# Expert routing made tile by tile, two routing tables, a gather issued one block earlier, and four edits in the first and the expert stage of a hybrid decoder layer

## The chip, the cores and the metric

One Trainium2 chip, one core of it. The metric is the device time of one execution in microseconds (us). TensorE is PE in the profile's rows, VectorE is DVE, ScalarE is ACT, GpSimd is POOL, and SyncE, which here only issues DMAs, is SP.

## What is computed

One decoder layer, 1024 tokens of width 1024, all float32. A recurrent branch and an attention branch share one input projection and one output projection; then each token goes to 4 of 32 experts.

```python
h = rmsnorm(x, ln1_w)
u, gate, q, k, v, f = split(h @ w_in)                      # 512, 512, 512, 512, 512, 8 columns
rec = rg_lru(conv4(u), ...) * gelu(gate)                   # a scan over the 1024 tokens
att = forgetting_attention(rmsnorm(q), rmsnorm(k), v, f)   # 8 heads of 64, causal
x = x + concat(rmsnorm(rec), rmsnorm(att)) @ w_out
h2 = rmsnorm(x, ln2_w)
top_vals, top_idx = top_k(h2 @ w_router + b_router, 4)     # of 32 experts
gates = softmax(top_vals)
for each expert e:                                         # over the tokens that chose it
    g = min(h2 @ w_gate_up[e][:, :1024] + b, 7)
    u = clip(h2 @ w_gate_up[e][:, 1024:] + b, -7, 7)
    x += gates * (((u + 1) * g * sigmoid(1.702 * g)) @ w_down[e] + b)
```

## The kernel before

The program is a row of blocks, one for each stage; a block ends when all its engines are done. Inside a block each engine has its own list of instructions, in the order in which the code is written, and they meet on semaphores (`wait_ge`, `then_inc`). `step(...)` issues an instruction and makes the same engine wait for its end.

**Stage A** (`stage_a`): the norm, the input projection in 20 chunks of 128 columns, and the recurrent branch. POOL issues 14 small DMAs for the parameters, then makes the identity and other constants (lines 188 to 215). PE waits for `consts` and all 14 DMAs before it transposes the parameters (line 543) and then the normed rows, 16 parts of 4 transposes, `turn(g)` (line 551), through two PSUM places. ACT takes each part as h_hi (line 267) and DVE as h_lo (line 411), and ACT's squares of the next row tiles stand between. Each product is three matmuls: hi with hi, hi with lo, lo with hi. From projection chunk 9 on `mean_squares` (line 579) sums the squares of a head pair, and behind chunks 10 to 13 `rec_squares` (line 586) adds up the squares of the four channel tiles of the recurrence with one float32 pair of matmuls each.

**Stage B** is the attention; the change does not touch it.

**Stage C** (`stage_c`): the output projection in 8 token tiles, the second norm and the router. PE: `project(t)`, `turn(t - 1)` (line 1121), `route(t - 2)` (line 1132), and at the end turn(7), route(6), route(7). DVE adds the residual (line 1076), scales to h2 (line 1081) and then adds the router's bias to the logits of tile t - 1 (line 1068), in one PSUM place.

**Stage D** (`stage_d`): the routing. DVE finds the best four experts of each tile (lines 1241 and 1242) and the choices as a 0/1 table (lines 1247 to 1250); PE counts them (lines 1331 to 1336). From the counts DVE works out how each expert's tokens are cut into work items of 256 down to 96 rows (classes of width), the experts' order (line 1277) and the list of items (line 1289), for which SP waits with the loads of the first expert's weights (six DMAs of 2 MB each). Then it finds the place of each token and builds, in 32 rounds, the two factors of a table (lines 1305 to 1308), whose products PE adds up (line 1342):

```python
            for q in range(TK):
                dve.tensor_scalar(one_lo[:, q, :], iota_lo[:], lo_f[:, q:q + 1], None, ALU.is_equal)
                dve.tensor_scalar(val_hi[:, q, 0, :], iota_hi[:], hi_f[:, q:q + 1], row_no[:, q:q + 1],
                                  ALU.is_equal, ALU.mult)
                dve.tensor_scalar(val_hi[:, q, 1, :], iota_hi[:], hi_f[:, q:q + 1], ex_q[:, q:q + 1],
                                  ALU.is_equal, ALU.mult).then_inc(lo_s, 1)
```

The sums are the token of each place (`rows_in`, line 1316) and its gate. Constants for all this come from POOL at the start of the block (line 1220).

**Stage E** (`stage_e`, once as E and once, only if numbers are out of range, as G): the experts. POOL clears `rows` (line 1547), copies two columns of `rows_in` (line 1522) and gathers 2 x 128 token rows by indirect DMA (line 1526). PE transposes them in four parts (line 1790), ACT and DVE split each part into x_hi and x_lo in float16 (lines 1594 and 1684), and weights are split alike, 256 columns at a time, into a ring of four (lines 1587 and 1664). Ahead of the loop ACT and DVE split four chunks of weights and then the four parts of the first rows. The loop has one body for each class of width, eight chunks of gate and up (lines 1823 to 1826) and four of down (line 1834) for each item; a weight slot is loaded again when its last use has gone.

## Time and profile before

| | us |
|---|---|
| median of 3 runs (lowest, highest) | 2110.95 (2109.69, 2113.56) |
| the profiled execution | 2106.65 |
| its span | 2104.9 |
| PE busy | 1938.3 |
| DVE busy | 1250.7 |
| ACT busy | 1049.5 |
| POOL busy | 400.0 |
| DMA | 501.73 MB, mean 238 GB/s |

An engine's busy time says how long it had an instruction in hand. Starts are given from the start of the span; a row of a timeline names in brackets how long its engine was idle before it, and what ended that. An idle engine costs something only where others wait for it.

### The profile page before, as it was taken

The numbers are of one execution on the slowest core, as the hardware profiler recorded it, in microseconds if no ns is written. First come the engines' busy times: TensorE is split into PE (matmuls) and PEld (weight loads), VectorE is DVE, ScalarE is ACT, GpSimd is POOL, SyncE is SP. The second block draws the span as 40 slices with busy tenths as digits, with TensorE's granted clock in tenths as the row PEclk, the third lists the DMA queues.
The fourth block names the chain that finished last, engine by engine and source line by source line (L and its number), as shares of the span: only waits on it lengthen the run. The fifth ranks groups of instructions, "written<-read, shape, count | busy, mean of one in ns | idle before, by whom it ended". The sixth has DMA issues, their size and how long they took to land.

```text
span 2104.9 us, 50349 instructions
## 1 busy us (share of the span) xinstructions
PE 1938.3 (92%) x20305; PEld 1790.2 (85%) x20305; DVE 1250.7 (59%) x2560; ACT 1049.5 (50%) x1444; POOL 400.0 (19%) x303
## 2 busy tenths in 40 slices
PE   6999998997964999999999999999999999998983
PEld 4777576786852999999999999999999999998982
DVE  4452345664247655555566667567868768677582
ACT  5464315552111444445555555556656566565561
POOL 4001000000002111111112211213324324233241
PEclk9999999998976999999999999999999999999996
DMA  4111102003429678888988899999999999999994
GB/s 136 41 40 40 31 2 80 1 1 133 151 78 327 201 268 279 276 277 290 306 300 271 287 300 337 336 337 299 354 372 359 367 370 355 370 363 361 370 352 119
DMA packets 251765, 501.73 MB, mean 238 GB/s; under 512 B 13024, under 2 KB 33808, under 8 KB 251584
## 3 DMA queue, kind: packets, MB, share of 16 engines
q1 hardware_dynamic: 231376, 446.73, 58.6%
q0 software_dynamic: 20256, 51.73, 11.3%
q10 hardware_dynamic: 48, 2.10, 0.3%
q8 instruction: 58, 0.95, 0.2%
q14 instruction: 27, 0.22, 0.0%
HBM read 471.16 MB, written 52.43 MB: 249 GB/s over the span
## 4 chain that ended last, share of the span: by engine, by line
PE 52%; DVE 4%; DMA 4%; issue 4%; SPq 2%; ACT 1%; POOL 0%; DVEq 0%; ACTq 0%; POOLq 0%
PE E_p_d L1834 22%; PE E_p_g L1823 5%; PE E_p_g L1826 5%; PE E_p_g L1825 5%; PE E_p_u L1826 4%; PE E_p_u L1823 4%; PE E_p_u L1825 4%; DMA E_w_st<-in_w_down 4%; DVE E_w_lo L1664 2%; PE E_p_t L1805 2%; PE E_p_t L1790 2%; SPq L1473 2%; ACT E_w_hi L1587 1%; DVE E_up L1724 0%; DVE E_gate L1712 0%
## 5 line engine op out<-in xcount | busy, mean ns | idle before, releaser
L1664 DVE SCALAR_TENSOR_TENSOR E_w_lo<-E_w_st,E_w_hi 128x2048 f16<-128x2048 f32 x260 | 594.6, 2287 | 61.8 <-ACT E_w_hi L1587 58.1
L1587 ACT ACTIVATE E_w_hi<-E_w_st 128x2048 f16<-128x2048 f32 x260 | 492.5, 1905 | 187.6 <-PE E_p_g L1826 98.6
L1834 PE MATMUL E_p_d<-E_a_f,E_w_st 128*128 128x160 f32 (+6 forms) x4096 | 537.0, 291 | 21.3 <-DMA E_w_st<-in_w_down 11.6
L1834 PEld LDWEIGHTS E_p_d<-E_a_f,E_w_st 128*128 128x128 f32 x4096 | 521.4, 193 | 29.3 <-DMA E_w_st<-in_w_down 12.6
L1823 PE MATMUL E_p_g<-E_x_hi,E_w_hi 128*128 128x160 f16 (+6 forms) x2048 | 373.1, 224 | 6.2 <-issue 6.2
L1823 PE MATMUL E_p_u<-E_x_hi,E_w_hi 128*128 128x160 f16 (+6 forms) x2048 | 371.7, 223 | 4.1 <-DVE E_w_lo L1664 4.1
L1825 PE MATMUL E_p_g<-E_x_lo,E_w_hi 128*128 128x160 f16 (+6 forms) x2048 | 373.1, 224 | 0.0
L1826 PE MATMUL E_p_g<-E_x_hi,E_w_lo 128*128 128x160 f16 (+6 forms) x2048 | 373.0, 224 | 0.0
L1826 PE MATMUL E_p_u<-E_x_hi,E_w_lo 128*128 128x160 f16 (+6 forms) x2048 | 371.7, 223 | 0.0
L1825 PE MATMUL E_p_u<-E_x_lo,E_w_hi 128*128 128x160 f16 (+6 forms) x2048 | 371.7, 223 | 0.0
L1536 POOL DMA_INDIRECT sum_rows<-E_y_rows,E_idx_out x66 | 169.1, 2562 | 598.7 <-ACT E_y_rows L1605 588.5
L1630 ACT ACTIVATE E_y_t<-E_p_d,E_bias 128x160 f32<-128x160 f32 (+6 forms) x256 | 81.7, 371 | 258.1 <-PE E_p_d L1834 258.1
L1823 PEld LDWEIGHTS E_p_g<-E_x_hi,E_w_hi 128*128 128x128 f16 x2048 | 201.0, 98 | 6.8 <-issue 6.7
L1823 PEld LDWEIGHTS E_p_u<-E_x_hi,E_w_hi 128*128 128x128 f16 x2048 | 200.4, 98 | 4.8 <-DVE E_w_lo L1664 4.8
L1825 PEld LDWEIGHTS E_p_g<-E_x_lo,E_w_hi 128*128 128x128 f16 x2048 | 201.0, 98 | 0.8
L1826 PEld LDWEIGHTS E_p_g<-E_x_hi,E_w_lo 128*128 128x128 f16 x2048 | 201.0, 98 | 0.1
L1825 PEld LDWEIGHTS E_p_u<-E_x_lo,E_w_hi 128*128 128x128 f16 x2048 | 200.4, 98 | 0.4
L1826 PEld LDWEIGHTS E_p_u<-E_x_hi,E_w_lo 128*128 128x128 f16 x2048 | 200.4, 98 | 0.0
L1703 DVE TENSOR_SCALAR E_bias<-bias 128x8 f32 x32 | 5.5, 172 | 285.6 <-ACT E_y_t L1630 283.4
L1526 POOL DMA_INDIRECT E_rows<-h_rows,E_idx_in x68 | 116.2, 1709 | 38.8 <-POOL E_idx_in L1522 28.5
L1712 DVE TENSOR_SCALAR E_gate<-E_p_g,E_bias 128x160 f32<-128x160 f32 (+6 forms) x256 | 79.5, 352 | 67.8 <-PE E_p_g L1826 67.8
L1622 ACT ACTIVATE E_sig<-E_gate 128x320 f32<-128x320 f32 (+6 forms) x128 | 54.8, 428 | 109.3 <-DVE E_gate L1712 108.1
(367 smaller groups left out, 2802.5 us busy)
## 6 DMA issues: line engine op xcount, KB each, us to landing
E_w_st<-in_w_gate_up SPq DMA_DIRECT2D x130, 2048.0 KB, 15.6
E_w_st<-in_w_down SPq DMA_DIRECT2D x64, 2048.0 KB
A_w_st<-in_w_in SPq DMA_DIRECT2D x20, 512.0 KB, 3.8
sum_rows<-C_x SPq DMA_DIRECT2D x10, 512.0 KB, 5.8
A_x_rows<-in_x SPq DMA_DIRECT2D x8, 512.0 KB, 8.6
B_wo_raw<-in_w_out SPq DMA_DIRECT2D x8, 512.0 KB, 3.2
C_x_res<-in_x SPq DMA_DIRECT2D x8, 512.0 KB, 4.2
x_rows<-C_x SPq DMA_DIRECT2D x8, 512.0 KB, 5.0
```

The lines of the kernel that those rows point to most:

```text
L1473: sp.dma_start(w_st[q][:], weights_of(a, e, q)).then_inc(w_in[q], 16)
L1526: pool.indirect_dma_start(rows[:, b, :], None, m.h2_d, bass.IndirectOffsetOnAxis(ap=idx_in[:, b:b + 1], axis=0), bounds_check=token_max, o ...
L1536: pool.indirect_dma_start(m.sum_d, bass.IndirectOffsetOnAxis(ap=idx_out[:, b:b + 1], axis=0), y_rows[:, b, :], None, bounds_check=row_max, ...
L1587: act.activation(w_hi[c % RI][:], staged(c % NG), ACT.Copy, scale=SW).then_inc(hi_s, 1)
L1622: act.activation(sig[j % 2][:, :, 0:w], gate[j % 2][:, :, 0:w], ACT.Sigmoid, scale=ALPHA / S1).then_inc(sig_s, 1)
L1630: ins = act.activation(y_t[:, 2 * j + h, 0:w], p_d[j % 2][:, h, 0:w], ACT.Identity, bias=bias[:, 16 + 2 * j + h:17 + 2 * j + h], scale=1.0 ...
L1664: dve.scalar_tensor_tensor(out=w_lo[c % RI][:], in0=staged(c % NG), scalar=SW, in1=w_hi[c % RI][:], op0=ALU.mult, op1=ALU.subtract, accum_ ...
L1712: ins = dve.tensor_scalar(gate[j % 2][:, h, 0:w], p_g[j % 2][:, h, 0:w], bias[:, 2 * j + h:2 * j + h + 1], S1 * LIMIT, ALU.add, ALU.min)
L1823: pe.matmul(o_, wh, x_hi[:, k, 0:w], start=h == 0 and k == 0, stop=False, skip_group_check=True)
L1825: pe.matmul(o_, wh, x_lo[:, k, 0:w], start=False, stop=False, skip_group_check=True)
L1826: ins = pe.matmul(o_, wl, x_hi[:, k, 0:w], start=False, stop=k == KT - 1, skip_group_check=True)
L1834: ins = pe.matmul(banks[:, h, 0:w], staged(c)[:, k, h * P:(h + 1) * P], x[:, k, 0:w], start=h == 0 and k == 0, stop=k == KT - 1, skip_grou ...
```

## The change

In stage A: the identity is made first on POOL and has a semaphore of its own; the two DMAs for `b_forget` and the forget weights are no longer among those that the parameter transpose waits for; `turn(g)` uses four PSUM places; the squares of the recurrence are added on DVE and summed by one pair of matmuls behind chunk 13. In stage C: the choices are made tile by tile on DVE, two tiles behind; the router's PSUM place is doubled; route(6) stands ahead of turn(7); the routing constants are made on POOL here. In stage D: fewer instructions for the counts, the table in two halves (tokens first, gates behind), `one_lo` in groups of eight, and the first gather. In stage E: the first gather and the clearing of `rows` are gone, and the first rows are split ahead of the weights, but for one weight split of ACT. Tables that live over stages have fixed places in memory.

```diff
@@ stage_a
+            step(pool.memset(m.ident[:], 0.0))
+            pool.affine_select(out=m.ident[:], ...).then_inc(ident_s, 1)
             for row, src in ((0, a.ln1_w[0]), ...):
-            pool.dma_start(bf[:], a.b_forget[0:1, :].to_broadcast([P, H])).then_inc(prm_in, 16)
+            pool.dma_start(bf[:], a.b_forget[0:1, :].to_broadcast([P, H])).then_inc(wf_in, 16)
-        N_PRM = 14 * 16
+        N_PRM = 12 * 16
...
+                if 10 <= n < 13:
+                    dve.wait_ge(rec_sq_s, n - 8)
+                    if n > 10:
+                        dve.wait_ge(rec_add, n - 10)
+                    dve.tensor_tensor(rec_all[:], rec_all[:], rec_sq[:], ALU.add).then_inc(rec_add, 1)
...
-            pe.wait_ge(consts, 1)
+            pe.wait_ge(ident_s, 1)
             pe.wait_ge(prm_in, N_PRM)
...
-                if g >= 2:
-                    pe.wait_ge(h_lo_s, g - 1)
+                if g == 3:
+                    pe.wait_ge(prm_s, 1)
+                if g >= 4:
+                    pe.wait_ge(h_lo_s, g - 3)
...
-                if 10 <= n < 10 + CT:
-                    rec_squares(n - 10)
+                if n == 13:
+                    rec_squares()
@@ stage_c
-                dve.tensor_tensor(m.logits[:, t, :], p_l[:], br_row[:], ALU.add).then_inc(log_s, 1)
+                dve.tensor_tensor(m.logits[:, t, :], p_l[t % 2][:], br_row[:], ALU.add).then_inc(log_s, 1)
+                dve.wait_ge(log_s, t + 1)
+                q = slice(TOPK * t, TOPK * (t + 1))
+                step(dve.max(m.top8[:, t, :], m.logits[:, t, :]))
+                step(dve.max_index(m.idx8[:, t, :], m.top8[:, t, :], m.logits[:, t, :]))
+                step(dve.tensor_copy(m.idx_f[:, q], m.idx8[:, t, 0:TOPK]))
+                step(dve.tensor_tensor(m.picked[:, q, :], ..., ALU.is_equal))
+                step(dve.tensor_reduce(m.chosen[:, t, :], ..., AX.X, ALU.add))
+                step(dve.tensor_copy(m.chosen_b[:, t, :], m.chosen[:, t, :]))
...
-                if t:
-                    logits(t - 1)
+                if t == 2:
+                    dve.wait_ge(tables, 1)
+                if t >= 2:
+                    logits(t - 2)
+            logits(T - 2)
             logits(T - 1)
@@ stage_d
+            pool.memset(m.first_rows[:], 0.0).then_inc(zeroed, 1)
+            pool.wait_ge(zeroed, 1)
+            pool.wait_ge(rows_in_s, 1)
+            pool.tensor_copy(m.first_idx[:], m.rows_in[:, 0:NB]).then_inc(idx_s, 1)
+            pool.wait_ge(idx_s, 1)
+            for b in range(NB):
+                pool.indirect_dma_start(m.first_rows[:, b, :], None, m.h2_d, ...).then_inc(m.gathered, 16)
...
+            for g in range(TK // GROUP):
+                w = slice(GROUP * g, GROUP * (g + 1))
+                dve.tensor_tensor(one_lo[:, w, :], ..., ALU.is_equal)
+                for q in range(GROUP * g, GROUP * (g + 1)):
+                    dve.tensor_scalar(val_row[:, q, :], m.iota_hi[:], hi_f[:, q:q + 1], m.row_no[:, q:q + 1],
+                                      ALU.is_equal, ALU.mult).then_inc(row_s, 1)
...
+            dve.tensor_copy(m.rows_in[:], ids_f[:]).then_inc(rows_in_s, 1)
             ex_q = ex[:].rearrange("p t k -> p (t k)")
             for q in range(TK):
+                dve.tensor_scalar(val_gate[:, q, :], m.iota_hi[:], hi_f[:, q:q + 1], ex_q[:, q:q + 1],
+                                  ALU.is_equal, ALU.mult).then_inc(gate_s, 1)
@@ stage_e
-                pool.memset(rows[:], 0.0).then_inc(cleared, 1)
-                pool.wait_ge(cleared, 1)
-                gather(0, 1)
+                if fast:
+                    pool.sem_inc(cleared, 1)
+                    pool.sem_inc(idx_s, 1)
+                    pool.sem_inc(gone_s, 1)
...
+                for g in range(NP):
+                    x_part(0, g, CHUNK)
+                    if fast and g == 1:
+                        act.wait_ge(w_in[slot(0)], 16)
+                        split_hi(0)
                 if fast:
-                    for c in range(RI):
+                    for c in range(1, RI):
...
-                    for c in range(RI):
-                        split_lo(c + 1, c)
                     for g in range(NP):
                         x_part(0, g, CHUNK)
+                    for c in range(RI):
+                        split_lo(c + 1, c, True)
```

PE at the end of stage C, behind the last matmul of `project(7)`, before (C_p_m is written by turn, C_p_l by route):

```order
L1121 MATMUL C_p_m<-ident,C_h_3939 128x128 x8
L1132 MATMUL C_p_l<-C_w_router,C_h2t_3936 128x32 x8
L1121 MATMUL C_p_m<-ident,C_h_3940 128x128 x8
L1132 MATMUL C_p_l<-C_w_router,C_h2t_3935 128x32 x8
L1132 MATMUL C_p_l<-C_w_router,C_h2t_3936 128x32 x8
```

The same place of the change:

```order
L1164 MATMUL C_p_m<-ident,C_h_3956 128x128 x8
L1175 MATMUL C_p_l<-C_w_router,C_h2t_3953 128x32 x8
L1175 MATMUL C_p_l<-C_w_router,C_h2t_3952 128x32 x8
L1164 MATMUL C_p_m<-ident,C_h_3957 128x128 x8
L1175 MATMUL C_p_l<-C_w_router,C_h2t_3953 128x32 x8
```

The last transposes have moved behind the routing of tile 6.

POOL from the start of stage E, before, and from the start of stage D, in the change:

```order
L1547 MEMSET E_rows 128x2048
L1522 COPY E_idx_in<-rows_in 128x2
L1526 DMA E_rows<-h_rows,E_idx_in 128x1024 x2
L1550 IOTA E_idx_out 128x2
L1552 MEMSET E_warm 128x1
```

```order
L1263 MEMSET first_rows 128x2048
L1266 COPY first_idx<-rows_in 128x2
L1269 DMA first_rows<-h_rows,first_idx 128x1024 x2
L1197 UNCONDITIONAL_BRANCH
L1557 UNCONDITIONAL_BRANCH
L1497 TENSOR_LOAD bounds
L1497 ISA x2
L1594 IOTA E_idx_out 128x2
```

The clearing, the index copy and the first gather now stand ahead of the branch into stage E.

ACT at the start of stage E, before and in the change (E_w_hi is a chunk of weights, E_x_hi a part of the rows):

```order
L1587 ACTIVATE E_w_hi_5410<-E_w_st_4882 128x2048
L1587 ACTIVATE E_w_hi_5411<-E_w_st_4883 128x2048
L1587 ACTIVATE E_w_hi_5412<-E_w_st_4882 128x2048
L1587 ACTIVATE E_w_hi_5413<-E_w_st_4883 128x2048
L1594 ACTIVATE E_x_hi<-E_p_t 128x4x128 x4
```

```order
L1638 ACTIVATE E_x_hi<-E_p_t 128x4x128 x2
L1631 ACTIVATE E_w_hi_5515<-E_w_st_5032 128x2048
L1638 ACTIVATE E_x_hi<-E_p_t 128x4x128 x2
L1631 ACTIVATE E_w_hi_5516<-E_w_st_5033 128x2048
L1631 ACTIVATE E_w_hi_5517<-E_w_st_5032 128x2048
L1631 ACTIVATE E_w_hi_5518<-E_w_st_5033 128x2048
```

All four row parts and their transposes no longer have four weight splits ahead of them, but one in their middle.

## Rows read from the trace of the kernel before

**Rows 1.** Busy time by stretch: length, each engine, clock, DMA share, GB/s.

```profile
core 0: us, PE busy (x) PEld busy (x) DVE busy (x) ACT busy (x) POOL busy (x), PEclk, DMA share, GB/s
600.00:610.00 10.00, 6.15 (x29) 6.05 (x29) 2.09 (x5) 2.44 (x5) 0.00 (x0) 0.55 0.39 157
613.00:662.00 49.00, 24.40 (x134) 14.83 (x134) 43.88 (x175) 2.32 (x3) 2.81 (x12) 0.71 0.64 228
...
688.00:1200.00 512.00, 512.00 (x5551) 509.68 (x5550) 307.73 (x616) 259.24 (x345) 77.82 (x70) 1.00 0.83 279
1690.00:2105.00 415.00, 353.07 (x5282) 347.00 (x5280) 272.09 (x578) 228.60 (x304) 135.36 (x72) 0.94 0.97 332
```

**Rows 2.** Timeline, start of stage A: start, duration, engine, instruction, idle before.

```profile
6.70 0.96 POOL L194 DMA_DIRECT2D A_prm_rows<-in_k_norm_w  x2
...
13.00 0.75 DVE L405 TENSOR_SCALAR A_x_rows<-A_x_rows,A_sm 128x1024 f32<-128x1024 f32 x1 [1.10 <-ACT A_sm L262]
...
15.28 0.31 PE L543 MATMUL A_p_g<-ident,A_prm_rows 50*128 50x50 f32 x1 [15.28 <-DMA A_wf_st<-in_w_in]
...
26.68 0.69 ACT L267 ACTIVATE A_h_hi<-A_p_g,prm 128x512 fp32r<-128x512 f32 x1 [0.55 <-PE A_p_g L551]
```

**Rows 3.** Timeline of PE, head sums behind three projection chunks of stage A.

```profile
168.98 1.89 PE L579 MATMUL A_p_g<-A_square,head_cols 128*16 128x512 f32 x4
...
181.95 1.89 PE L579 MATMUL A_p_g<-A_square,head_cols 128*16 128x512 f32 x4
...
196.57 1.89 PE L579 MATMUL A_p_g<-A_square,head_cols 128*16 128x512 f32 x4
```

**Rows 4.** Timelines of PE and DVE, end of stage C.

```profile
596.11 1.03 PE L1121 MATMUL C_p_m<-ident,C_h 128*128 128x128 f32 x8
...
603.47 1.97 PE L1121 MATMUL C_p_m<-ident,C_h 128*128 128x128 f32 x8 [4.62 <-DVE C_h L1081]
...
609.07 3.59 PE L1132 MATMUL C_p_l<-C_w_router,C_h2t 128*128 128x32 f32 x16 [0.38 <-DVE logits L1068]
...
599.07 1.23 DVE L1076 TENSOR_TENSOR C_x<-C_p_o,C_x_res 128x1024 f32<-128x1024 f32 x1
...
612.70 0.19 DVE L1068 TENSOR_TENSOR logits<-C_p_l,C_br_row 128x32 f32<-128x32 f32 x1 [3.78 <-PE C_p_l L1132]
```

**Rows 5.** Timelines of PE and DVE in stage D.

```profile
616.77 1.91 PE L1325 MATMUL D_p_b<-ident,D_bgu_rows 32*128 32x32 f32 x16 [4.10 <-DMA D_bd_rows<-in_b_down]
...
628.69 0.59 PE L1339 MATMUL D_p_eid<-ident,D_eid 128*1 128x128 f32 x2 [5.97 <-DVE D_eid L1277]
...
622.82 0.19 DVE L1257 COPY D_cnt<-D_p_cnt 128x32 f32<-128x32 f32 x1 [1.03 <-PE D_p_cnt L1336]
...
631.16 0.20 DVE L1289 CAST items<-D_p_eid 1x50 int32<-1x50 f32 x1
...
636.70 0.29 DVE L1305 TENSOR_SCALAR D_one_lo<-D_iota_lo,D_lo_f 128x128 f32<-128x128 f32 x1
...
637.14 0.33 DVE L1308 TENSOR_SCALAR D_val_hi<-D_iota_hi,D_hi_f,D_ex 128x98 f32<-128x98 f32 x1
...
660.29 0.21 DVE L1316 CAST rows_in<-D_ids_f 128x98 uint32<-128x98 f32 x1
```

**Rows 6.** Timelines from D's end to the first expert matmul, and the source view of the gather.

```profile
664.40 2.23 POOL L1522 COPY E_idx_in<-rows_in 128x2 uint32<-128x2 uint32 x1
...
682.35 0.18 POOL L1522 COPY E_idx_in<-rows_in 128x2 uint32<-128x2 uint32 x1 [5.85 <-PE E_p_t L1790]
...
664.30 2.29 DVE L1664 SCALAR_TENSOR_TENSOR E_w_lo<-E_w_st,E_w_hi 128x2048 f16<-128x2048 f32 x1 [1.64 <-ACT E_w_hi L1587]
...
677.71 1.97 PE L1790 MATMUL E_p_t<-ident,E_rows 128*128 128x128 f32 x8 [18.59 <-DMA E_rows<-h_rows,E_idx_in]
...
687.80 0.34 PE L1823 MATMUL E_p_g<-E_x_hi,E_w_hi 128*128 128x192 f16 x1 [5.52 <-issue]
...
L1526 POOL DMA_INDIRECT E_rows<-h_rows,E_idx_in x68: 1003/1093/3124, 667.5 to 2055.4; - x68
...
DMA to landing us min/median/max: 3.5/7.4/9.6
```

More of the change, by code:

```diff
@@ L266, in h_part @@
                 act.wait_ge(turned, g + 1)
-                act.activation(h_hi[:, k, half * 512:(half + 1) * 512], p_g[g % 2][:, 0, :], ACT.Copy,
+                act.activation(h_hi[:, k, half * 512:(half + 1) * 512], p_g[g % 2][:, g // 2 % 2, :], ACT.Copy,
                                scale=ln1[:, k:k + 1]).then_inc(h_hi_s, 1)
@@ L1160, in at @@
             off = place[0]
-            place[0] += -(-n // 64) * 64
-            assert place[0] <= 186 * KIB
+            for lo, hi in gaps:
+                if off < hi and off + n > lo:
+                    off = hi
+            place[0] = off + -(-n // 64) * 64
+            assert place[0] <= 186 * KIB - 8 * KIB or off >= 181 * KIB or place[0] <= 180 * KIB
             return nc.alloc_sbuf_tensor_at("D_" + name, shape, dt, offset=m.base + off)
@@ L1174, in stage_d @@
-        tri, ones_b = at("tri", [P, P], BF16), at("ones_b", [P, P], BF16)
-        cnt, full, rem, part = (at(n, [P, E_], F32) for n in ("cnt", "full", "rem", "part"))
+        ex, esum = at("ex", [P, T, TOPK], F32), at("esum", [P, T], F32)
+        cnt, full, rem = (at(n, [P, E_], F32) for n in ("cnt", "full", "rem"))
+        four = at("four", [P, S // CHUNK, E_], F32)
         base_full, jump, full_rows = (at(n, [P, E_], F32) for n in ("base_full", "jump", "full_rows"))
-        limit = at("limit", [P, NV + 1], F32)
@@ L1253, in _ @@
-            step(dve.reciprocal(esum[:], esum[:]))
-            step(dve.tensor_tensor(ex[:], ex[:], esum[:].unsqueeze(2).to_broadcast([P, T, TOPK]), ALU.mult))
-            dve.wait_ge(pos_mm, 2)
-            step(dve.tensor_copy(cnt[:], p_cnt[:]))
-            step(dve.tensor_scalar(full[:], cnt[:], float(CHUNK), None, ALU.is_ge))
-            for q in range(2, S // CHUNK + 1):
-                step(dve.tensor_scalar(part[:], cnt[:], float(q * CHUNK), None, ALU.is_ge))
-                step(dve.tensor_tensor(full[:], full[:], part[:], ALU.add))
@@ L1262, in _ @@
-            step(dve.tensor_scalar(full_rows[:], full[:], float(CHUNK), None, ALU.mult))
-            step(dve.tensor_tensor(rem[:], cnt[:], full_rows[:], ALU.subtract))
+            dve.wait_ge(pos_mm, 1)
+            step(dve.tensor_copy(cnt[:], p_cnt[:]))
+            step(dve.tensor_tensor(four[:], cnt[:].unsqueeze(1).to_broadcast([P, S // CHUNK, E_]),
+                                   m.fulls[:].unsqueeze(2).to_broadcast([P, S // CHUNK, E_]), ALU.is_ge))
+            step(dve.tensor_reduce(full[:], four[:].rearrange("p q e -> p e q"), AX.X, ALU.add))
@@ L1277, in _ @@
             dve.tensor_copy(eid[:], eid_i[:]).then_inc(eid_s, 1)
-            step(dve.tensor_copy(m.bounds[:], upto[0:1, :, E_ - 1]))
+            step(dve.tensor_scalar(full_rows[:], full[:], float(CHUNK), None, ALU.mult))
             step(dve.tensor_tensor(start[:], upto[:], share[:], ALU.subtract))
@@ new lines, in _ @@
+            dve.wait_ge(ex_s, 1)
+            step(dve.tensor_reduce(esum[:], ex[:], AX.X, ALU.add))
+            step(dve.reciprocal(esum[:], esum[:]))
+            step(dve.tensor_tensor(ex[:], ex[:], esum[:].unsqueeze(2).to_broadcast([P, T, TOPK]), ALU.mult))
+            dve.wait_ge(row_mm, 1)
+            step(dve.tensor_copy(raw[:], p_row[:]))
+            step(dve.tensor_scalar(far[:], raw[:], 0.0, float(FAR), ALU.is_equal, ALU.mult))
+            step(dve.scalar_tensor_tensor(out=ids_f[:], in0=raw[:], scalar=-1.0, in1=far[:], op0=ALU.add, op1=ALU.add))
@@ L1318, in _ @@
+            step(dve.tensor_tensor(sums_f[:], ids_f[:], m.spare[:].rearrange("p a b -> p (a b)"), ALU.min))
             step(dve.tensor_copy(m.rows_out[:], sums_f[:]))
+            step(dve.tensor_copy(m.bounds[:], upto[0:1, :, E_ - 1]))
+            dve.wait_ge(gate_mm, 1)
+            step(dve.tensor_copy(m.gates[:], p_gate[:]))
         @block.tensor
         def _(pe):
+            for t in range(T):
+                ins = pe.matmul(p_cnt[:], m.ones_b[:], m.chosen_b[:, t, :], start=t == 0, stop=t == T - 1)
@@ L1322, in _ @@
+            ins.then_inc(pos_mm, 1)
+            for t in range(T):
+                ins = pe.matmul(p_pos[:, t, :], m.tri[:], m.chosen_b[:, t, :], start=True, stop=t == 0)
+                for s_ in range(t):
+                    ins = pe.matmul(p_pos[:, t, :], m.ones_b[:], m.chosen_b[:, s_, :], start=False, stop=s_ == t - 1)
+            ins.then_inc(pos_mm, 1)
             pe.wait_ge(bias_in, 32)
@@ L1340, in _ @@
             for q in range(TK):
-                pe.wait_ge(lo_s, q + 1)
-                ins = pe.matmul(p_tab[:].rearrange("p a b -> p (a b)"), one_lo[:, q, :],
-                                val_hi[:, q, :, :].rearrange("p a b -> p (a b)"), start=q == 0, stop=q == TK - 1)
-            ins.then_inc(tab_mm, 1)
+                pe.wait_ge(row_s, q + 1)
+                ins = pe.matmul(p_row[:], one_lo[:, q, :], val_row[:, q, :], start=q == 0, stop=q == TK - 1)
+            ins.then_inc(row_mm, 1)
+            for q in range(TK):
+                pe.wait_ge(gate_s, q + 1)
+                ins = pe.matmul(p_gate[:], one_lo[:, q, :], val_gate[:, q, :], start=q == 0, stop=q == TK - 1)
+            ins.then_inc(gate_mm, 1)
 NSLOT = 6
```

217 lines of the change are left out of this document (118 added, 99 removed).

## The prediction

> **What bounds the kernel now.** I read the busy table by stage first: which stretches does TensorE not fill? From 688 to 1200 us it is busy all the time at a full clock, with the DMA engines at 0.83; in the last 415 us it has gaps and the DMA share is 0.97; between 613 and 662 us it is busy for half the time at 0.71 of its clock [rows 1]. So the long expert stage is bound by matmuls, later by weight loads, and each expert's loads start when matmuls free a slot. Work ahead of its first matmul at 687.80 is worth its full time, if that chain is what starts it. The timelines say it is: PE waits 18.59 us for the first gathered rows (677.71), the gather waits for the row table (660.29), the table for counts and choices that VectorE (DVE) makes one after the other, and these for the last logits at 612.70 [rows 4 to 6]. The first stage is filled by PE from about 16 us on, so there it is PE's own instructions and its start that count [rows 2, 3].
>
> **Stage A, start.** The parameter transpose waited until 15.28 for the constants and the last of 14 parameter DMAs [rows 2]. Now the identity comes first on POOL (some 1.2 us, by which each DMA behind it is issued later) and only 12 DMAs are waited for. The last k_norm issue began at 7.19 (two in the row) and took about 4.9 us to land: 13.3 us now. The normed rows are ready at 13.00 + 0.75. PE so turns from 13.8 instead of 15.52: 1.7 us. Four PSUM places instead of two let PE run ahead in the eight parts of the first half; ScalarE waited 0.55 us there in such a part [rows 2], in about four of eight: a gain of 0 to 1.8 us, taken as 1.1, since ScalarE and DVE are nearly full there. **2.8 us.**
>
> **Stage A, recurrence norm.** PE's period from one head sum to the next is 12.97 us without the matmuls over rec_sq and 14.62 with them [rows 3]. Four become one: 3 x 1.65 = **5.0 us**. DVE's three adds of 1.23 us lie in its idle time inside PE's 13 us; were that cover gone they would cost 3.7 us. The one sum still ends at the same place, so the reciprocal behind it is not later.
>
> **Stage C, end.** DVE held the last residual add until 599.07, behind the logits of tile 6; project(7) ends at 596.1 [rows 4]. Logits now run two tiles behind, so the add starts at 596.4. ScalarE must first copy tile 6 away (it does so from 597.2 to 598.3) before it squares tile 7, so h2 of tile 7 comes 2.0 us earlier: turn(7) at 601.45 instead of 603.47. route(6) has moved in front of it, into time in which PE waited 4.62 us. Then turn 1.0, copies 1.1, route(7) 1.9 at the full clock, and DVE's seven steps (about 0.25 each, as the small steps of rows 5) 1.75: the end is at 607.6 instead of 612.89, **5.3 us**. Before, the eight transposes took 1.03 us behind project(7) and 1.97 us behind the gap, where the granted clock was 0.55 on average, and the last route took 3.59, twice what I take [rows 1, 4]. The new gap is 0.6 us, so I take the full clock; if it still falls to its lower level, 2.6 us are lost. The six new DVE steps of the other tiles (1.6 us) are covered by 11 us of project(t).
>
> **Stage D, the table.** Old: from the block's start (613.2) to the end of rows_in (660.5), 47.3 us. New, by rows of the same kind [rows 5]: the top-8 and choices are done, so the count is read 0.7 us after the start instead of 9.6: -8.9. Counting up to the expert ids was 5.8 us (622.82 to 628.63); ten small instructions become four: -1.1. PE has the bias transposes ahead of the id matmul; they waited for their DMA until 3.6 us after the start and take 2.8, so the ids come at 7.0, while DVE has 1.1 us of other work: +0.6. The 32 rounds were 0.20 + 0.24 + 0.24 = 0.68 us each (one_lo and one value row in 0.44), 21.8; now 4 x (1.23, as the 1024-wide add of rows 4, + 8 x 0.24) = 12.4: -9.3. The tail: -0.3. Sum **19.0 us**: 28.3 us from start to rows_in. The item list, for which the first weight loads wait, is written at +7.2 instead of +18.2 (631.16 and its 0.20).
>
> **The gather.** The index copy on POOL began 3.9 us after rows_in, behind the block change and the clearing of the rows; now POOL waits for it: **3.8 us**. From copy to landing it was 13.3 us: 2.24 of copy, two issues, then transfer [rows 6]. The ends: the second issue lands 3.5 to 9.6 us after it starts, an issue takes 1.0 to 3.1 us, the copy 0.2 to 2.2. I take 12.2, near the old value, for the loads of 12.6 MB are still running, and count **1.1 us**. Block D ends 8.5 us after rows_in (gate table 32 x 0.24, then 0.9), and E begins 1.5 us later, 10.0 after the copy: hidden by the landing.
>
> What stands against this is DVE's gate table, which now runs beside POOL's copy and descriptors. The row shows the danger: the copy of two indices took 2.24 us beside an E_w_lo split of 2.29 that began 0.1 us before [rows 6], whereas a later one takes 0.18. The Trainium skill (SBUF — State Buffer, Who interferes with whom) says that DVE and GpSimd share one port pair as an exclusive lock, taken by a tensor_scalar in two-port mode, and that descriptors cannot be written meanwhile. The trace agrees for the copy; no row shows whether 32 short instructions let POOL in between. By that rule the gain on the gather would be some 5 us less, the first rival.
>
> **Stage E, start.** From landing to first matmul it was 687.80 - 677.71 = 10.1 us; transposes 4.6, then 5.5 of PE's own class branches [rows 6]. The weight splits, formerly under the wait for rows, now come behind them: the row parts end 6.0 + 0.7 (one ScalarE split lies between them), the first w_lo 2.5 later: 9.2 after landing. Cover by 0.9 us, so **0**. Chunks 1 to 3 need one more each at 2.5 us while PE takes 6.5 and then 4.4 per chunk. DVE enters the loop 10 us later relative to the rows, yet chunk 4 starts only 29 us after landing and needs its split at 22.5.
>
> **Sum.** 2.8 + 5.0 + 5.3 + 19.0 + 3.8 + 1.1 = 37.0 us. The profiled execution took 2106.65 us (span 2104.9): 2069.6. It lies 4.3 us under the median of the runs, 2110.95, so for that median I forecast **2074.0 us**.
>
> **Rivals.**
> - Port lock: POOL gets in only when the gate table is done, 7.7 us after rows_in. Copy, gap and two issues at their short prices (3.3), then the usual flight: landing 5.5 us later than forecast, 2079.5. For: the 2.24 us copy. Against: gaps between instructions of 0.24 us. 16%.
> - Several small terms fail (clock in C's end 2.6, parameters late 1.5, parts not denser 1.1): 2079. 10%.
> - Better: the loads end before the branches of E, and PE's 5.5 us shrink or the clock rises earlier in stage A; the landing is at E's start, 2 us earlier: 2069. 10%.
> - Given back in the load-bound end: if the weight queue were full all along, only the start of the first load would count, 11.0 + 5.3 us, and stage A's 7.8: 24, hence 2087. Against: DMA share 0.83 from 688 to 1200 [rows 1]. 5%.
> - Slower: the clock does not rise in the first expert. With ACT and DVE still splitting, PE's chunks 1 to 3 could be spaced so that 1.2 GHz stays for the whole item of 52 us, which becomes about 104; +52 - 37 = +15, 2126. It decides from 0.7 of an item at half rate. Against: before, PE was at its full clock some 5 us into the first chunk, and the new waits there are covered. 2%.
> - The change does not do what it says: the gather is held by something else (its flight behind the first 12.6 MB in full, until about 653 + 1). Then 5.5 us are lost as with the lock: 3%.
>
> The forecast itself has 54%. Its own spread is 2069 to 2079. The range of 2065 to 2084 takes in the first three rivals and the runs' spread of some 2 us each way, and leaves out some 9%. A measurement of this kernel can tell 0.2%, 4 us: faster 0.96, same 0.02, slower 0.02.
>
> **What would show it.** In the profile after: first transposes at 13.8; only one head-sum period with the extra matmuls; the last logits end near 600; rows_in near 628.4, POOL's index copy right behind it with a duration of 0.2 to 2.2; first gathered rows turned near 640.7; first expert matmul near 650.8, and every later item earlier by the same 37. It is wrong if the first expert matmul is early and the end is not (loads), if PE waits for E_w_lo in the first item, or if the copy starts more than a few us behind rows_in.

## The result, and the profile after

| | before | changed |
|---|---|---|
| median of 4 runs, us | 2110.4 (2109.69 to 2113.56) | 2073.14 (2070.18 to 2076.04) |
| ratio | | 0.9821, 95% interval 0.9803 to 0.9838 |
| profiled execution, us | 2106.65, span 2104.9 | 2076.04, span 2074.2 |

The medians lie 37.3 us apart, the two profiled executions only 30.7: that of before was 3.0 us faster than the fastest of its four runs, that of the changed kernel was the slowest of its four. The first thing to settle is therefore where these 6.6 us sit, before a term of the forecast is read off two traces. The page of the changed kernel shows the same kernel, shorter ahead of the experts:

```profile
PE 1935.6 (93%) x20357; PEld 1798.3 (87%) x20357; DVE 1255.5 (61%) x2558; ACT 1049.2 (51%) x1444; POOL 397.8 (19%) x304
...
PEclk9999999998977999999999999999999999998997
DMA  4111102003438788888999899999999999999993
```

Stage A, timeline of PE in the changed kernel (start, duration, engine, instruction, idle before): the row turns, three head sums, the first matmul of the V projection.

```profile
13.25 6.20 PE L563 MATMUL A_p_g<-ident,A_x_rows 128*128 128x128 f32 x28
...
165.90 1.89 PE L591 MATMUL A_p_g<-A_square,head_cols 128*16 128x512 f32 x4
178.86 1.89 PE L591 MATMUL A_p_g<-A_square,head_cols 128*16 128x512 f32 x4
191.81 1.89 PE L591 MATMUL A_p_g<-A_square,head_cols 128*16 128x512 f32 x4
...
255.32 0.79 PE L674 MATMUL A_p_in<-A_v_hi,A_h_hi 128*128 128x512 f32 x1 [4.04 <-DVE A_v_lo L385]
```

The head sums are 12.95 to 12.97 us apart, where 14.62 stood with the extra matmuls [rows 3], and the first is 3.1 us earlier. The end of stage C, timeline of PE, then of DVE:

```profile
590.86 1.03 PE L1164 MATMUL C_p_m<-ident,C_h 128*128 128x128 f32 x8
591.73 3.66 PE L1175 MATMUL C_p_l<-C_w_router,C_h2t 128*128 128x32 f32 x32
596.05 1.97 PE L1164 MATMUL C_p_m<-ident,C_h 128*128 128x128 f32 x8 [0.66 <-DVE C_h L1121]
...
599.19 3.62 PE L1175 MATMUL C_p_l<-C_w_router,C_h2t 128*128 128x32 f32 x16 [1.18 <-ACT C_h2t L1076]
```
```profile
602.92 0.19 DVE L1099 TENSOR_TENSOR logits<-C_p_l,C_br_row 128x32 f32<-128x32 f32 x1 [3.24 <-PE C_p_l L1175]
```

Two router groups ran at the full clock (3.66 us for 32 matmuls). The last transposes, which stand behind them after only 0.66 us of idle time, and the last router group did not: 1.97 and 3.62 us, as before the change [rows 4]. From stage D's table to the first expert matmul, timelines of all engines:

```profile
633.49 0.21 DVE L1348 CAST rows_in<-D_ids_f 128x98 uint32<-128x98 f32 x1
633.86 0.19 POOL L1266 COPY first_idx<-rows_in 128x2 uint32<-128x2 uint32 x1 [26.69 <-DVE rows_in L1348]
634.63 1.13 POOL L1269 DMA_INDIRECT first_rows<-h_rows,first_idx  x1 [0.58 <-POOL first_idx L1266]
636.07 1.03 POOL L1269 DMA_INDIRECT first_rows<-h_rows,first_idx  x1 [0.30 <-issue]
...
642.13 0.26 DVE L1357 COPY gates<-D_p_gate 128x98 f32<-128x98 f32 x1
645.12 0.36 SPq L1515 DMA_DIRECT2D E_ln<-in_ln_w  x1
646.06 1.96 PE L1843 MATMUL E_p_t<-ident,E_rows 128*128 128x128 f32 x8 [4.06 <-PEq L1197]
646.11 0.07 DVE L1745 MEMSET E_total_all<- 128x8 f32 x1 [3.72 <-PEq L1197]
...
652.44 2.28 DVE L1717 SCALAR_TENSOR_TENSOR E_w_lo<-E_w_st,E_w_hi 128x2048 f16<-128x2048 f32 x1
...
654.86 0.34 PE L1876 MATMUL E_p_g<-E_x_hi,E_w_hi 128*128 128x192 f16 x1 [4.24 <-DVE E_w_lo L1717]
```

rows_in comes 28.4 us behind the block's start, the copy behind it at once and in 0.19 us, the issues in 1.13 and 1.03 us beside DVE's gate table. Two things are new. Between DVE's last copy of stage D and the next block lie 3.7 us, where it was 1.5. And the first expert matmul is put down to E_w_lo, the case that the forecast named as a sign of being wrong. Both were tested.

The first scatter of every expert item shows what became of the gain: 32.64 us ahead of before at item 0, 32.62 at item 10, 32.62 at item 25, then 29.4 to 33.1, and 30.91 at the last. So what is gained ahead of the first expert matmul (32.9) stays unchanged for 1100 us, and only the last seven items, which wait for weight loads, move by some 3 us.

### The profile page after: what moved, and what is told of

Its sections match the earlier page's. It is cut to its first block, busy times and chain, and to the rows that moved or that the text cites. A ratio compares the mean times of both kernels' runs of the same rounds, so it can differ in the third digit from the quotient of the medians.

```text
span 2074.2 us, 50459 instructions
## 1 busy us (share of the span) xinstructions
PE 1935.6 (93%) x20357; PEld 1798.3 (87%) x20357; DVE 1255.5 (61%) x2558; ACT 1049.2 (51%) x1444; POOL 397.8 (19%) x304
## 4 chain that ended last, share of the span: by engine, by line
PE 53%; DVE 4%; issue 4%; DMA 4%; SPq 2%; ACT 1%; DVEq 0%; POOL 0%; ACTq 0%; POOLq 0%
PE E_p_d L1887 22%; PE E_p_g L1876 5%; PE E_p_g L1878 5%; PE E_p_g L1879 5%; PE E_p_u L1876 4%; PE E_p_u L1879 4%; PE E_p_u L1878 4%; DMA E_w_st<-in_w_down 4%; DVE E_w_lo L1717 2%; SPq L1512 2%; PE E_p_t L1858 2%; PE E_p_t L1843 2%; ACT E_w_hi L1631 1%; DVE E_up L1777 0%; DVE E_gate L1765 0%
## 5 line engine op out<-in xcount | busy, mean ns | idle before, releaser
L1887 PEld LDWEIGHTS E_p_d<-E_a_f,E_w_st 128*128 128x128 f32 x4096 | 523.9, 194 | 28.5 <-DMA E_w_st<-in_w_down 12.6
```

The lines of the kernel that those rows point to most:

```text
L1887: ins = pe.matmul(banks[:, h, 0:w], staged(c)[:, k, h * P:(h + 1) * P], x[:, k, 0:w], start=h == 0 and k == 0, stop=k == KT - 1, skip_grou ...
```

## Experiments

Ten kernels and a second profile of each of the two, each timed beside the kernel before. Since executions of one kernel start up to 1 us apart, intervals within a trace are compared, mostly from turn(6), PE's transposes of tile 6 behind project(7), or from stage D's first matmul. Where a time is given as so much more than the changed kernel, its second median, 2074.89, is meant.

### The two kernels again

> The kernel before, unchanged, for a second profile. Theory (the time up to the 26th item is fixed and the last six items, which wait for weight loads, vary by some microseconds; the first profile of before was a lucky end): first expert matmul within 1 us of 687.80 and the first scatter of item 26 within 1 us of 1808.6, but the last scatter 2 to 7 us behind the 2072.45 of the first profile. Rival (the difference of the medians, larger than that of the two profiles, comes from earlier stages): the first expert matmul itself moves by 3 us or more.

> The changed kernel, unchanged, for a second profile and for a time beside the other variants on one chip. Theory: first expert matmul within 1 us of 654.86, and 32 to 33.5 us ahead of that of the second profile of before; the last six items again differ by up to 3 us from the first profile. Rival: the first profile's 32.9 us were themselves chance, and the two second profiles differ by 36 us or more at the first expert matmul.

2112.68 us (2109.35 to 2114.39) and 2074.89 us (2074.11 to 2075.33), ratio 0.9820 (0.9803 to 0.9836). Starts in us, gain from one profile to the other:

| | before | changed | gain | before again | changed again | gain |
|---|---|---|---|---|---|---|
| rows turned, stage A | 15.52 | 13.25 | 2.3 | 16.11 | 13.84 | 2.3 |
| first head sum above | 168.98 | 165.90 | 3.1 | 169.47 | 165.75 | 3.7 |
| last head sum | 257.53 | 249.38 | 8.2 | 258.02 | 249.23 | 8.8 |
| stage B, first matmul | 314.58 | 307.93 | 6.7 | 316.60 | 307.51 | 9.1 |
| stage C, first matmul | 479.99 | 474.51 | 5.5 | 483.18 | 474.09 | 9.1 |
| turn(6) | 596.11 | 590.86 | 5.3 | 599.54 | 590.25 | 9.3 |
| stage D, first instruction | 613.21 | 605.34 | 7.9 | 616.64 | 604.74 | 11.9 |
| rows_in | 660.29 | 633.49 | 26.8 | 663.73 | 632.68 | 31.1 |
| first gathered rows turned | 677.71 | 646.06 | 31.7 | 680.36 | 645.16 | 35.2 |
| first expert matmul | 687.80 | 654.86 | 32.9 | 691.34 | 654.14 | 37.2 |
| scatter of item 25 | 1808.60 | 1775.98 | 32.6 | 1812.26 | 1775.24 | 37.0 |
| last scatter | 2072.45 | 2041.54 | 30.9 | 2076.38 | 2040.92 | 35.5 |

My theory of a lucky end fell; both rivals hold. The first profile of before is 3.5 us ahead at the first expert matmul, and only 0.4 us are added behind it; and the second pair lies 37.2 us apart there. 2.7 of the 3.5 us arise at two places, from the first V matmul to stage B (51.1 against 52.7 us) and from there until DVE has read its first scores (5.6 against 6.8 us), both stretches in which PE starts again behind a wait. Windows of the second profile of before (length, PE busy, granted clock, DMA share, GB/s):

```profile
260.00:265.00 5.00, 1.05 (x3) 0.83 0.00 0
265.00:270.00 5.00, 5.00 (x13) 0.50 0.00 0
```

PE is busy from 265 to 270 at half its clock, 1.2 GHz. In the first profile of before only the V projection's first six matmuls took 0.63 us or more; here it was 13, and 13 in the first profile of the changed kernel too. I had read this as a cost of the change; it varies from execution to execution. Of the 13 profiles with no filler there, ten have 11 to 13 such matmuls, before's first has six, and w0_in_d and fill_e have seven; the 5.6 us behind stage B's start stand in before's first profile alone.

### Stage A alone

```diff
-(stage_a of the kernel before)
+(stage_a of the changed kernel; all else as before)
```

> The kernel before with stage A of the changed kernel, and nothing else. Theory (two waits of TensorE are followed by more matmuls at the low clock, at the start of the V projection and of the attention, and give 2.7 us back): the last head sum moves from 257.53 to about 249.4, stage C's first project matmul from 479.99 only to about 474.5, the first expert matmul from 687.80 to about 682.3, and the median lies 5.5 us under that of before. Rival (the low clock after those waits belongs to the one profiled execution): stage C starts near 472.2 and the median lies 7.8 us under before.

2104.17 us against 2113.8, ratio 0.9957 (0.9940 to 0.9974): 9.6 us. First expert matmul at 682.17, 9.2 us ahead of the second profile of before. The median went the rival's way, and by more than its 7.8 us. The starts in the trace went the theory's way: stage C begins at 473.92 and the first expert matmul is within 0.2 us of the 682.3 named, because PE is at the low clock behind both waits here too (11 matmuls of 0.63 us or more at the first). What was wrong in the theory was its base, the unusual first profile of before. Against the second one, stage A's part arrives in full.

### The gather back in stage E

```diff
-(stage D: POOL's memset, index copy and two gathers)
 def run():
+    pool.memset(rows[:], 0.0).then_inc(cleared, 1)
+    pool.wait_ge(cleared, 1)
+    gather(0, 1)
```

> The changed kernel with the first gather back in stage E (memset, index copy and both gathers behind the block change), rows still split ahead of weights. Theory (the block change is held because POOL has a gather under way, not by the next block's code): behind DVE's last copy of stage D at 642.4 the next block starts 1.5 us later as before the change, not 3.7; rows then land near 655.6, 8.8 us later comes the first expert matmul, near 664.4 against 654.86, and the time is 2082 to 2084. Rival 1 (the longer block change has nothing to do with the gather): 3.7 us again, first expert matmul near 666.5. Rival 2 (VectorE's work makes the index copy slow): the copy takes 0.2 us here, because VectorE is idle while it waits for the rows, against 2.2 us in the kernel before, where it stood beside the splits; if the copy is slow by itself in this block it takes 2.2 us here too.

2082.93 us, 8.0 more than the changed kernel. Timeline of DVE, then of POOL:

```profile
643.00 0.26 DVE L1344 COPY gates<-D_p_gate 128x98 f32<-128x98 f32 x1 [1.22 <-PE D_p_gate L1369]
644.72 0.07 DVE L1727 MEMSET E_total_all<- 128x8 f32 x1 [1.46 <-PEq L1197]
```
```profile
646.56 0.18 POOL L1548 COPY E_idx_in<-rows_in 128x2 uint32<-128x2 uint32 x1
647.63 1.13 POOL L1552 DMA_INDIRECT E_rows<-h_rows,E_idx_in  x1 [0.89 <-POOL E_idx_in L1548]
```

The block change is 1.46 us again, so the gather held it. And the copy takes 0.18 us where it took 2.22 to 2.25 in this block in before's two profiles and in a_only [rows 6]; what is gone is the split beside it.

### Gate table ahead of the row numbers

```diff
+for q in range(TK):
+    dve.tensor_scalar(val_gate[:, q, :], ...)
 dve.wait_ge(row_mm, 1)
 ...
 dve.tensor_copy(m.rows_in[:], ids_f[:]).then_inc(rows_in_s, 1)
-for q in range(TK):
-    dve.tensor_scalar(val_gate[:, q, :], ...)
```

> The changed kernel with the 32 multiplications for the gate table ahead of the row numbers again, so that the tables are split but the gather isn't early. Theory (the block change follows the gather by 9.0 us behind its second issue, and each of the 32 takes 0.24 us): rows_in comes 36 us instead of 28.4 behind stage D's start, the gather, the block change and the first expert matmul 7.7 us later, and the time is 7.7 us longer. Rival (VectorE has the same work up to the end of stage D in either order, and the block change must wait for that anyway): the first expert matmul comes 4 us later or less.

2082.89 us, 8.0 more; first expert matmul 56.4 us behind stage D's first matmul instead of 49.4. DVE's timeline:

```profile
641.62 0.26 DVE L1357 COPY gates<-D_p_gate 128x98 f32<-128x98 f32 x1
652.37 0.07 DVE L1745 MEMSET E_total_all<- 128x8 f32 x1 [10.49 <-PEq L1197]
```

DVE, done, waits 10.5 us for the block change. From POOL's second issue (643.34) to the new block's first instruction on DVE it is 9.0 us here and 10.0 in the changed kernel (636.07 to 646.11), whatever DVE does. What it follows is the landing. The source views of the two issues (POOL, changed kernel and this one) say how long each took to land:

```profile
DMA to landing us min/median/max: 7.2/8.0/8.7
```
```profile
DMA to landing us min/median/max: 7.2/7.5/7.7
```

The second gather lands at 644.75 in the changed kernel and at 651.02 here, and DVE's first instruction of the new block follows 1.36 and 1.35 us later. It is 1.34 to 1.37 us in all seven profiles in which the gather lands last. Where DVE ends last (w0_in_d, w0_and_banks, fill_e) the block begins some 1.5 us behind DVE, as it does without a gather. Splitting the tables is worth 7 to 8 us, all of it through the gather's time.

### The end of stage C

```diff
-route(T - 2)
 turn(T - 1)
+route(T - 2)
 route(T - 1)
```

> The changed kernel with one line of stage C's end moved back: the last transposes stand ahead of the router matmuls of tile 6, which so fall at the low clock behind them. Theory (TensorE's clock is at its low level from the last transposes on, whatever the order): the last transposes stay near 596.05 and take 1.97 us, both router groups take 3.6 us each behind them, the last logits come 2.4 us later (605.3 instead of 602.9), and the time is 2.4 us longer. Rival (the clock fell because the narrow router matmuls ran ahead of the last transposes): the transposes and routers run at the full clock in 1.0 and 1.9 us and the last logits come no later than 602.9.

2076.88 us, 2.0 more. Timeline of PE:

```profile
594.74 1.97 PE L1164 MATMUL C_p_m<-ident,C_h 128*128 128x128 f32 x8 [2.44 <-DVE C_h L1121]
596.50 6.88 PE L1175 MATMUL C_p_l<-C_w_router,C_h2t 128*128 128x32 f32 x32
```

Last logits 13.9 us behind turn(6) instead of 12.1: 1.9. That is the theory's mechanism and nearly its size. In the trace the 1.9 us still stand at the first expert matmul, but the first scatter is only 0.9 us later (79.7 us behind turn(6) instead of 78.8).

Nor is it the length of the gap that decides. Windows of the changed kernel, then of the kernel before, from turn(6) on (length, PE busy, clock, DMA share, GB/s):

```profile
590.86:595.86 5.00, 4.53 (x41) 1.00 0.52 210
595.95:600.86 4.91, 3.64 (x16) 0.50 0.26 107
```
```profile
596.11:600.91 4.80, 2.74 (x25) 1.00 0.00 0
600.95:606.11 5.16, 2.64 (x13) 0.50 0.76 305
```

In both the clock falls about 5 us behind turn(6), though PE had then been idle for 0.5 us in the one and for 2.0 us in the other. It falls 4.8 to 5.1 us behind it in 13 of 14 profiles and 6.5 us behind it in late_gather. What all have in common is that PE has only transposes and 128x32 router matmuls, or nothing, to do behind the wide matmuls of project(7); whether the narrow work alone brings the clock down no run tests.

### Weights first

```diff
-(rows' parts, then the four weight splits, on ACT and DVE)
+(the four weight splits, then the rows' parts)
```

> The changed kernel with only the order of the first splits in stage E undone: four weight splits ahead of the rows on ScalarE and VectorE. Theory (the rows are ready when the block starts, so what is put first on VectorE sets the first matmul): four weight splits end near 657.4, the rows' low parts near 662.6, first expert matmul near 662.7, that is 7.8 us later than in the changed kernel, and the time near 2081. Rival (the first item catches up, since later weight splits are then already done): the first matmul is late but the first item's end is not, and the time is within 2 us of the changed kernel's.

2086.32 us, 11.4 more, and 11.8 at the first expert matmul (665.94), though DVE finished the low parts of the rows near 660.5, earlier than I said. PE stood idle behind them "until issue". The source view of the line `with eng.If(hi > lo)` (durations in ns: least, median, most) shows why, here:

```profile
L1487 PEldq COMPARE_BRANCH  x2: 83/3146/6208, 658.5 to 665.4; - x2
```

and in the first profile of the changed kernel:

```profile
L1487 PEldq COMPARE_BRANCH  x2: 83/1753/3423, 650.2 to 654.3; - x2
```

The class of 256 rows is empty for these inputs. PE's sequencer jumps over the unrolled loop of that class, and this one branch takes 6.21 and 3.42 us; the next, not taken, 0.083. The first expert matmul comes 1.26 to 1.33 us behind the end of this branch in all 14 profiles, whatever the splits do, so it is the branch that ends the wait. PE's one other jump over a long unused part of the program, stage G, behaves alike: 3.32 to 3.76 us in the 14 profiles, at a DMA share of 0.02 to 0.03. The Trainium skill (Advanced Engine Details and Errata, Control Flow Timing) gives a compare-and-branch some 108 ns, which the branch not taken comes near and the taken one does not. The Trainium skill (Runtime: NRT & Kernel Launch, Instruction fetch mechanics) also says that a taken branch beyond the instructions at hand must first fetch its target by DMA. DMA traffic should then lengthen it.

### The branch beside DMA traffic

```diff
 sp.dma_start(ln2[:], ...)
+for half in range(2):      # 2 MB, input x to output, overwritten in the last stage
+    sp.dma_start(a.out[0, 256 * half:256 * half + 256, :], a.x[0, ...]).then_inc(busy_s, 16)
```

> The changed kernel with a copy of 2 MB from the input x into the output (overwritten at the end) started by the SP queue at the start of stage E; nothing of the computation waits for it before the last item. Theory (what ends TensorE's wait before the first expert matmul is its branch over the loop of the empty class, whose instructions come by DMA: 3.4 to 3.7 us in the runs where the DMA engines are idle then, 4.6 to 6.2 us where weight loads fill them): the branch takes 5 to 6 us instead of 3.4, the first expert matmul comes 1.8 to 2.6 us later behind the first transposes (8.8 in the changed kernel, 10.6 to 11.4 here), and the time is 2.2 us longer. Rival (the longer branches belong to the old order of the splits and not to DMA traffic): 3.4 us and the same time.

2078.02 us, 3.1 more; the first expert matmul 12.5 us behind the first transposes instead of 8.8 to 9.0. The branch took 7.08 us, more than the 5 to 6 expected. Its time in all 14 profiles and the DMA share while it ran:

| kernel | branch, us | DMA share |
|---|---|---|
| changed (both), late_gather, turn_first, w0_in_d, fill_v, gate_first | 3.42 to 3.66 | 0.05 to 0.22 |
| before, first profile | 4.62 | 0.96 |
| fill_e | 4.99 | 0.53 |
| before again | 5.51 | 0.99 |
| a_only | 5.56 | 0.99 |
| w0_and_banks | 5.94 | 0.58 |
| weights_first | 6.21 | 1.06 |
| busy_branch | 7.08 | 0.77 |

Only the direction is shown, not a law for the size: at shares of 0.53 to 0.77 the branch took anything from 5.0 to 7.1 us. It explains the 1.3 to 2.0 us which the change gained unforeseen: rows first means that the next expert's loads, which wait for the third weight split, start at 658.7 instead of 674.9, but the branch now runs ahead of them, and in before it ran in their midst.

### Looking for a faster version

```diff
 (stage D, ACT)   act.activation(m.bias[:], ...)
+                 act.activation(m.w_hi0[:], m.w_st[0][:, :, 0:256], ACT.Copy, scale=2.0 ** 8)
 (stage D, DVE, behind the gate table)
+                 dve.scalar_tensor_tensor(out=m.w_lo0[:], in0=m.w_st[0][:, :, 0:256], ...)
```

> The changed kernel with the first weight column split in stage D: ScalarE takes its high part behind the bias copy, VectorE its low part behind the gate table. Theory (in the changed kernel the first expert matmul waits for that low part, 652.44 to 654.74, and the block change is held by the gather, so that 2.5 us more of VectorE in stage D cost at most 0.3 us): the block starts near 646.4, the rows' low parts are ready near 652.0, the first expert matmul comes near 652.1 instead of 654.86, and the time is 2.5 us under the changed kernel's. Rival 1 (the block change follows VectorE's end, not the gather): it starts 2.5 us later, at 648.6, and nothing is gained. Rival 2 (TensorE must wait for the second column anyway): the first matmul is early and the first scatter is not.

The split of this column in stage E is gone, and the gate table takes the memory of the token table. 2073.64 us; the first scatter 79.0 us behind turn(6), as in the changed kernel (78.8): no gain, as rival 2 would have it, but by another mechanism. PE's row: 

```profile
652.80 0.34 PE L1883 MATMUL E_p_g<-E_x_hi,E_w_hi 128*128 128x192 f16 x1 [4.32 <-issue]
```

The same wait, 8.9 us behind the first transposes, though the first E_w_lo was long done: in the changed kernel the split and the wait set by the branch had ended together.

```diff
-pe.transpose(p_t[g % 2][...], rows[...], m.ident[:])
+pe.transpose((p_d if early and g >= 2 else p_t)[g % 2][...], rows[...], m.ident[:])
```

> The kernel with the first weight column split in stage D (w0_in_d), and the first item's third and fourth transpose groups turned into the banks of the down projection, which are free, so that TensorE waits for nobody between them and reaches its branch sooner. Theory (the branch, and not the low part of the weights, ends the wait, as w0_in_d without a gain suggests): the branch starts 2.8 us behind the first transposes instead of 4.1, the first expert matmul 7.5 instead of 8.9 us, and the time is 1.1 to 1.4 us under the changed kernel's. Rival (the rows' low parts end the wait once the weights are early): they are ready 5.0 us behind the first transposes, so this would show only under 5.5 us; or the branch simply ends at the same time whatever comes ahead, and nothing is gained.

2071.6 us, ratio 0.9804 (0.9787 to 0.9822). The branch began 0.7 us behind the first transposes and took 5.94 us, since the first expert's last loads were still landing; the matmul came after 8.0 us instead of 8.9, and the first scatter 76.8 us behind turn(6), 2.0 less.

```diff
+pe.wait_ge(w_in[4], 16)
+for n in range(2):      # result unread, ahead of the branch
+    pe.matmul(p_u[1][...], m.ident[:], w_st[4][:, n, 0:512], start=True, stop=True)
```

> The kernel w0_and_banks with two matmuls of 128x512 in f32 whose result nobody reads, behind the first item's transposes and ahead of the branch. Theory (TensorE works on them while its sequencer is in the branch; an idle stretch there is what the low clock of the first item's first 5 us follows, as it was at the V projection): they take about 1.7 us each and end before the branch does, the first expert matmul stays 8.0 us behind the first transposes, but fewer of the first item's matmuls run at the low clock and the first scatter comes 1 to 2.6 us earlier than in w0_and_banks (76.8 us behind the turn of tile 6). Rival 1 (3.4 us of work are not enough, or the low clock here comes from the narrow work of the whole of stage D): the same 76.8 us. Rival 2 (the filler holds the branch or the matmuls up): later by 1 us or more. For the time as a whole the theory gives 2069 to 2071, either rival 2071 to 2073.

2070.81 us (2070.29 to 2072.13), ratio 0.9798 (0.9785 to 0.9811): 4.1 us under the changed kernel's second median, with intervals that just overlap; in the traces 3.7 us from turn(6) to the first scatter (75.1), and kept up to item 25. Against w0_and_banks that is 1.7 us in one profile of each, and 0.8 us in the medians, with runs that overlap. Timeline of PE:

```profile
648.27 2.27 PE L1880 MATMUL E_p_u<-E_w_st,ident 128*128 128x512 f32 x4
652.55 0.25 PE L1890 MATMUL E_p_g<-E_x_hi,E_w_hi 128*128 128x192 f16 x1 [2.01 <-issue]
```

and its windows from the block's start on (length, PE busy, clock, DMA share, GB/s):

```profile
644.90:648.90 4.00, 4.00 (x17) 0.50 0.94 341
648.90:652.90 4.00, 1.99 (x9) 0.98 0.20 45
652.90:654.90 2.00, 2.00 (x27) 1.00 0.64 229
```

The first item starts at the full clock, 2.4 GHz, 0.25 us a matmul where it was 0.34 to 0.37 for its first 5.9 us in the changed kernel. The first expert matmul itself comes only 0.3 us sooner behind the first transposes than in w0_and_banks; the other 1.4 of the 1.7 us arise inside the first item, where the clock is what differs.

### The clock at the V projection

```diff
+for n in range(15):      # result unread, in the wait for v_lo
+    pe.matmul(p_in[1][:, 1, :], h_hi[:, n % KT, 0:P], h_hi[:, n % KT, 0:512], ...)
 pe.wait_ge(wlo_s, NW)
```

> The changed kernel with 15 matmuls of 128x512 whose result nobody reads put into TensorE's wait of 4.04 us ahead of the V projection. Theory (that wait is what the low clock follows, and the V projection's first 13 to 14 matmuls at 0.63 instead of 0.39 us are the 1.5 us that the change lost there): the V projection's first matmul stays near 255.3, all its matmuls take 0.39 us, its end and stage C's start come 2.8 us earlier, and so does everything up to the last items; the time is 2.8 us under the changed kernel's. Rival (the low clock comes from something else than an idle TensorE): the same 13 matmuls at 0.63 us and the same time.

2074.12 us, within 0.8 of the changed kernel. Windows of PE:

```profile
255.00:260.00 5.00, 4.90 (x21) 1.00 0.00 0
...
305.00:310.00 5.00, 5.00 (x12) 0.50 0.46 144
```

Right on the cause: with PE kept busy the V projection runs at the full clock and stage B's first matmul comes at 304.90 instead of 307.51. Wrong on the worth: behind the block change the low clock comes back and lasts longer, DVE reads its first scores 8.5 us behind that matmul instead of 6.8, and stage C starts only 0.3 us earlier.

## Why the prediction was right, term by term

2074.0 was forecast, 2073.1 measured. The terms, by both pairs of profiles. The second pair lies 36.0 us apart in its spans (2109.5 and 2073.5), near the medians' 37.3 and, of the runs of these two kernels on that chip, 37.8 (38.9 by the other thirteen runs of before there); the first pair 30.7. Rows are rounded, sums are not:

| term | forecast | second pair | first pair |
|---|---|---|---|
| stage A, start | 2.8 | 3.7 | 3.1 |
| recurrence norm | 5.0 | 5.1 | 5.1 |
| from there to turn(6) | 0 | 0.5 | -2.9 |
| stage C, end | 5.3 | 2.6 | 2.6 |
| stage D, table | 19.0 | 19.2 | 18.9 |
| gather | 4.9 | 4.2 | 4.9 |
| stage E, start | 0 | 2.0 | 1.3 |
| behind the first expert matmul | 0 | -1.7 | -2.0 |
| sum | 37.0 | 35.5 | 30.9 |

- **Stage A**: the step is right; the start gave 0.3 to 0.9 us more. The rows were turned 2.3 us earlier in both pairs, where 1.7 were forecast (the last parameter landed at 12.9 and 12.5 instead of 13.3), and the four places gave 0.8 and 1.4 us more up to the first head sum, where 1.1 were forecast.
- **"The new gap is 0.6 us, so I take the full clock"** failed: the gap was 0.66, and the clock fell all the same, ahead of the last transposes in nine of ten profiles with this order of stage C's end, and within them in the tenth (late_gather: 1.09 us, but 3.62 for the router group behind them). The 2.6 us named for that case are what is missing. The step took the gap for the cause, while the clock fell as late behind turn(6) as it had before the change. The terms written down for this end add up to 607.2, not 607.6; the 0.4 us have no source.
- **Stage D** is right to 0.2 us: sums over rows of the same kind carried it. (Four times 1.23 + 8 x 0.24 make 12.6 us, not 12.4; 12.3 were measured.)
- **"Block D ends 8.5 us after rows_in and E begins 1.5 us later: hidden by the landing"** failed as a step, and luck made its time right. The gather landed 10.9 us after the copy began, 1.3 us sooner than forecast, and the block change that it holds then took 1.3 us more; the rows were turned 12.2 us after the copy, as forecast.
- **The port lock**, the first rival at 16%, did not come: 0.19 us for the copy beside 32 short multiplications. Beside a split with two inputs in SBUF the copy does wait, as the pair of 2.23 us in before and 0.18 in late_gather shows. The Trainium skill (SBUF — State Buffer, Who interferes with whom) says this of a DVE instruction with two SBUF inputs against one of GpSimd that reads SBUF; the traces agree, and the forecast had not taken up that part of the rule.
- **Stage E's start**: I had 5.5 us for PE's class branches from the trace and took them as fixed, and asked only whether DVE fits in. They shrank by 1.3 to 2.0 us; the rival "better" had that mechanism, with 10%. The wait named E_w_lo, but taking it away gained nothing; it is the branch that ends it.
- **The base**: the sum went against an execution 3.5 us ahead of a usual one, and adding the distance to the median repaired that unseen. Five errors (clock at C's end -2.7, the end -1.7, branch +2.0, start +0.9, before turn(6) +0.5) mostly cancel; so the number is better than the argument.

Open: what in stage C's end brings the clock down, and how the branch's time depends on traffic.

## What to carry to other kernels

Take a second profile of the unchanged kernel before reading small differences stage by stage. Intervals between landmarks inside each trace, against such a pair, show which term moved. Where a wait ends at a semaphore and at the sequencer's own branch at once, taking away the one gains nothing: look at the branch rows too. And a block's end waits until a gather issued in it has landed, so issue it as early as its indices allow.

## What was not expected of the hardware

- A taken branch of PE's sequencer over a long unused part of the program took 3.3 to 3.8 us in quiet, at both places where the program has one, and up to 7.1 us beside DMA traffic; the same branches on ACT or POOL took 0.05 to 0.06 us.
- With a gather under way, the next block's engines started 1.34 to 1.37 us behind the landing of its second half, 9.0 to 10.0 us behind the issue, even where DVE then stood idle for 10.5 us.
- Work that nobody reads, put into PE's waits, moved the clock as meant in both places. Ahead of the experts, where PE is busy for long after, it was worth 1.7 us in the one pair of traces; ahead of stage B it was worth 0.3.
